# Scores of a pair ahead of the turn before it, and split multiply-adds, in the attention stages of a two-layer hybrid block

## The reference

```
def block(qi):                                   # global attention
    s = jnp.einsum('bqgrd,bkgd->bgrqk', qi, k_all).astype(jnp.float32) * d ** -0.5
    p = jax.nn.softmax(s, axis=-1).astype(v_all.dtype)
    return jnp.einsum('bgrqk,bkgd->bqgrd', p, v_all)
...
y = g[:, :, 0] * (branches[0] @ w_branch[0])     # merge
for i in range(1, N_BRANCH):
    y = y + g[:, :, i] * (branches[i] @ w_branch[i])
return y @ w_out
...
mod = jax.nn.silu(c) @ w_mod[l] + b_mod[l]       # modulation of a layer
```

## Time and profile before

| | us |
|---|---|
| median of 3 runs | 2744.23 |
| lowest and highest | 2742.33, 2746.5 |
| the profiled execution | 2742.03 |
| its span | 2740.4 |

### The profile page before, as it was taken

The page is one execution under the profiler, slowest core; times in us unless marked ns, Lnnn a source line. Parts: engine busy times, 40 slices in busy tenths (PEclk is TensorE's granted clock), DMA queues, the critical chain, the costliest instruction groups (busy, mean ns, idle before and its releaser), DMA issues.

```text
span 2740.4 us, 45413 instructions
## 1 busy us (share of the span) xinstructions
PE 2502.4 (91%) x19000; PEld 1530.5 (56%) x19001; DVE 1038.0 (38%) x2398; ACT 491.3 (18%) x978; POOL 231.8 (8%) x391
## 2 busy tenths in 40 slices
PE   7999999999998969999999999999999878888874
PEld 3455545454443457777777655667676544444442
DVE  2226536256465342222222251636457432111112
ACT  2023222222222011111111021323222111101110
POOL 3000001000000001111111110000000011111111
PEclk9989999999999979999999999999999979999997
DMA  9111118242324359999999762123465769999994
GB/s 293 61 62 62 47 43 305 114 142 85 112 87 131 125 193 370 370 374 381 378 383 387 292 203 92 62 77 104 145 185 179 257 265 409 410 418 413 415 404 169
DMA packets 153139, 616.72 MB, mean 225 GB/s; under 512 B 17121, under 2 KB 21489, under 8 KB 136465
## 3 DMA queue, kind: packets, MB, share of 16 engines
q1 hardware_dynamic: 126850, 557.88, 54.4%
q0 software_dynamic: 26192, 57.51, 6.5%
HBM read 598.37 MB, written 46.31 MB: 235 GB/s over the span
## 4 chain that ended last, share of the span: by engine, by line
PE 71%; DMA 15%; DVE 9%; issue 2%; ACT 2%; POOL 0%; DVEq 0%; SPq 0%; POOLq 0%; ACTq 0%
DMA ring<-in_e_down_dram 14%; PE bank L1660 13%; PE bank L1396 12%; PE bank L1288 11%; PE bank L1278 7%; PE score_banks L1677 4%; PE bank L1409 4%; PE score_banks L1697 3%; PE score_banks L1682 2%; PE bank L1567 2%; PE score_banks L1445 2%; PE turned_banks L1455 2%; PE bank L1643 1%; PE bank L1469 1%; PE bank L1317 1%
## 5 line engine op out<-in xcount | busy, mean ns | idle before, releaser
L1660 PEld LDWEIGHTS bank<-scr,ring 128*64 128x64 f32 x8192 | 340.6, 137 | 14.2 <-issue 14.2
L1396 PE MATMUL bank<-HT,ring 128*128 128x512 f32 (+1 forms) x1024 | 347.4, 494 | 0.8 <-ACT scr L1004 0.4
L1660 PE MATMUL bank<-scr,ring 128*64 128x96 f32 x8192 | 346.7, 247 | 1.2 <-DVE scr L2382 1.2
L1288 PE MATMUL bank<-ring,HT 128*128 128x512 f32 (+1 forms) x800 | 303.0, 535 | 0.0
L1653 PE MATMUL bank<-ring,scr 128*64 128x256 f32 x2048 | 239.8, 388 | 44.5 <-DMA ring<-in_e_gate_dram 22.8
L1396 PEld LDWEIGHTS bank<-HT,ring 128*128 128x128 f32 x1024 | 192.1, 192 | 143.2 <-issue 130.9
L1288 PEld LDWEIGHTS bank<-ring,HT 128*128 128x128 f32 x800 | 151.6, 193 | 142.3 <-issue 136.3
L1653 PEld LDWEIGHTS bank<-ring,scr 128*64 128x64 f32 x2048 | 146.5, 139 | 141.4 <-DMA ring<-in_e_gate_dram 41.5
L1278 PE MATMUL bank<-HT,ring 128*128 128x512 f32 (+1 forms) x512 | 196.1, 542 | 1.8 <-ACT HT L1004 1.8
L1697 PE MATMUL score_banks<-ring,scr 128*64 128x512 f32 x512 | 133.7, 670 | 35.5 <-DMA ring<-in_e_down_dram 33.8
L1278 PEld LDWEIGHTS bank<-HT,ring 128*128 128x128 f32 x512 | 97.0, 192 | 91.9 <-issue 88.4
(11 more groups left out here) (267 smaller groups left out, 2715.7 us busy)
## 6 DMA issues: line engine op xcount, KB each, us to landing
ring<-in_e_up_dram SPq DMA_DIRECT2D x64, 2048.0 KB, 22.0
ring<-in_e_down_dram SPq DMA_DIRECT2D x64, 2048.0 KB, 20.9
ring<-in_e_gate_dram SPq DMA_DIRECT2D x64, 2048.0 KB, 21.2
ring<-in_w_in_dram SPq DMA_DIRECT2D x34, 2048.0 KB, 8.0
ring<-in_w_mod_dram SPq DMA_DIRECT2D x32, 1024.0 KB, 5.2
ring<-in_w_mod_dram SPq DMA_DIRECT2D x8, 2048.0 KB, 19.5
ys<-consts POOLq DMA_DIRECT2D x1, 12288.0 KB, 41.7
ring<-in_w_branch_dram SPq DMA_DIRECT2D x4, 2048.0 KB, 7.9
```

Of the source, the lines that this page charges most:

```text
L1288: m = pe.matmul(bank[:, 0:width], HT[:, k, t * P:t * P + P], w[:, k, 0:width], start=k == 0, stop=k == KT_D - 1)
L1396: m = pe.matmul(bank[:, 0:NQ], w[:, k, (ft % 4) * P:(ft % 4) * P + P], HT[:, k, 0:NQ], start=k == 0, stop=k == KT_D - 1)
L1660: m = pe.matmul(ps[bank][rows_, f * cap:f * cap + cap], w[:, k, f * P + hf * HALF:f * P + hf * HALF + HALF], XTv[:, k, :], start=k == 0, s ...
```

## The change

On TensorE scores(i) now stands ahead of turn(i-1) in each step. On VectorE the part of the modulation sums that belongs to a step is cut in two by a new function `piece`: up to two multiply-adds (none in the first step of a block) go between peaks(i) and normalise(i), the rest stays at the end of the step. No wait is added or removed.

```diff
                     for i in range(n + 1):
+                        if i < n:
+                            scores(i)
                         if i:
                             turn(i - 1)
-                        if i < n:
-                            scores(i)
...
+                    def piece(b, i, late):
+
+                        for j in range(len(sum_blocks(l, b))):
+                            first, last = sum_span(l, b, j)
+                            ops, width = sum_list(l, b, j), last - first
+                            if not first <= i < last:
+                                continue
+                            part = ops[len(ops) * (i - first) // width:len(ops) * (i - first + 1) // width]
+                            early = 0 if i == first else min(2, len(part) // 2)
+                            part = part[early:] if late else part[:early]
+                            if part:
+                                accumulate(b, j, part)
+
                     for i in range(n + 1):
                         if i < n:
                             peaks(i)
+                            piece(b, i, 0)
                             normalise(i)
...
-                        for j in range(len(sum_blocks(l, b))):
-                            first, last = sum_span(l, b, j)
-                            ops, width = sum_list(l, b, j), last - first
-                            part = ops[len(ops) * (i - first) // width:len(ops) * (i - first + 1) // width] if first <= i < last else []
-                            if part:
-                                accumulate(b, j, part)
+                        piece(b, i, 1)
```

## The result

| | before | changed |
|---|---|---|
| median, us | 2745.36 (4 runs, 2742.33 to 2749.89) | 2702.2 (4 runs, 2698.78 to 2706.89) |
| the profiled execution | 2742.03 | 2698.78 |
| its span | 2740.4 | 2697.3 |
| granted TensorE clock of it | 0.959 | 0.961 |

The ratio is 0.9841, 95% interval 0.9824 to 0.9859: 43.2 us faster, where 31.6 was forecast. The kind of change was right and its size was a quarter too small.

The account below looks back on a forecast made before the run. TensorE, busy 91% of the span, was taken to bound the kernel; shorter waits and regained clock sum to 31.6 us, so 2742.0 becomes 2710.4, plus 2.2 for the median 2712.6, say 2713 us; range 2705 to 2732.

Parts of the forecast that it names:

- The idle terms: The waits to be removed in stages D, B and C of both layers, without the clock: 27.4 us.
- Scores followed by a turn never occur in before: TensorE's new neighbour order in 66 swapped steps, absent from the earlier trace; its price or gain was taken as 0.
- Its two bounds: Order on TensorE: losing a 0.07 us overlap in 66 steps costs 4.6 us, gaining as much is possible.
- the rule: Trainium skill: a weight load overlaps running matmuls only if they use other row groups; would make the gain smaller, not followed.
- three of its slow stretches: Stage C of layer 0: three stretches at lowered TensorE clock return to the upper level, 1.4 us each, 4.2.
- four places: Start of D, second long wait there, the 4.82 us wait, the 3.3 of layer 1: clock assumed to stay low.
- rival B: The clock stays up everywhere, also where the forecast left it slow: up to 8 us more, 2705 us; chance 0.05.
- the start of D: Layer 0: first turn waits 3.96 us, following group 2.03 for ScalarE; scores first to give 3.0, clock left slow.
- the 4.82: Longest turn wait, in C of layer 0, 4.82 us: only 1.1 was to go, and its clock to stay low.
- The turn's entry: TensorE's waits before a pair's transposes for VectorE's division, 38.7 us in 21 pieces; forecast to fall to about 10.
- Rival A: A new wait replaces the old as VectorE stays behind: gain only 12 to 16.6 us, 2727.6 to 2732; chance 0.23.

Follow-up runs that it names:

- scores first alone: Kernel before with only TensorE's list changed, scores(i) ahead of turn(i-1), multiply-adds left at the step's end: 2721.95 us against 2745.78, ratio 0.9916.

## Why the prediction was right, and where it was wrong

**Right.** That TensorE's idle time bounds the kernel and that the turn's waits are what the edit reaches: all 42.9 us are in the six stages. The idle terms (27.4 forecast, 24.0 measured), by stage: D 5.2 against 3.9, B 4.7 and 4.7, C 9.7 and 8.6, layer 1 7.8 and 6.8 (1.9, 1.6 and 3.3). The 0.6 us that the values' wait grows by in three steps of C: 0.63 each. That no multiply-add waits for its block: L2043 has no wait for a transfer. That multiply-adds beside exponentials cost nothing: the median L2043 takes 747 ns in both kernels, an exponential (L1165) 677 and 676. That scores to turn takes less than 1.2 us for a wide pair: 1.06. That the experts' stages take as long and only start earlier.

**Wrong, first: "Scores followed by a turn never occur in before ... I take 0".** The order was worth about 6.6 us (1.8 of them measured alone, in B of layer 0). Its two bounds, 4.6 us either way, came from the overlap of 0.07 us of two neighbours, and the value lies outside them. That overlap was also misread as a hidden load ("so I do not follow the rule"): at turn to scores and at scores to group the load starts together with its matmul, 0.00 us ahead, though the rows overlap by 0.07; where it is hidden, from turn to group, they overlap by 0.16 (1.09 busy, 0.93 apart). The rows that price it were there: a turn behind a dense group takes 0.97 us to the next start and 1.02 behind values, and its weight load starts 0.43 us early behind the group and not at all behind values. I looked at the edges that the new order makes, of which before has none, and not at the edges that it takes away or at the loads. Of the 44 edges from scores to a group in layer 0, each with an exposed load, the edit removed 41.

**Wrong, second: the clock, "three of its slow stretches stay at the upper level, 1.4 each: 4.2".** It is 10.7. I counted it in one stage only and left four places slow (rival B had them at up to 8 us together). Most of those recovered in part: the group behind the start of D took 8.80 us and takes 7.10, the one behind the 4.82 took 8.74 and takes 7.73. Waits that only became shorter give back clock too. Rival B had the second error's size nearly right (8 against 6.5) and a chance of 0.05, which was too low: there was no reason in the rows why a wait cut from 3.96 to 2.85 should keep its whole price.

**The sum.** Forecast 31.6; add 6.6 for the order and 6.5 for the clock, take off 3.4 for the waits: 41.3, against 42.9 in the stages and 43.2 of the medians. Had the two terms been right, the forecast would have been within 2 us.

**Smaller misses.** The turn's entry was to fall to about 10 us; it is 2.5, and the 12.4 stand under the scores' name, which the text did not foresee (14.9 together). L2195 and L2196 were to lose 32 of their 72 waits for ScalarE; they lost 15 (17 and 40 are left). Their waiting time fell from 101.1 to 64.8 us. The gate groups of C were to take 7.13 us; behind a turn they take 7.03, and one, behind the longest wait, 7.73. Rival A, "VectorE stays behind", is what scores first alone does (waits in B from 4.7 to 3.3); with the multiply-adds early it didn't happen.

**What stays open.** Order and clock come to 17.3 of the 18.9 us of busy time; the rest isn't explained. 0.6 of it is in C of layer 1, which lost 1.2 us at a clock of 1.00 in both, where the loads give 0.6. B of layer 0 gained 0.6 us and not the 0.9 that the rows give when scores went beside values. The order's value was measured apart from waits and clock in two stages only; for the others it is the estimate from their steps. Why a load isn't started early where the shape changes, no run here shows.

## What to carry to other kernels

When an edit only reorders a saturated TensorE, list the pairs of neighbours that it makes and that it removes, and look in the weight-load rows for which of them hide a load (here those of the same shape); with dozens of repetitions a load of 0.19 us is a term of the sum. Price a wait with the slow matmuls behind it, and let that price shrink with the wait. Work that is moved into another engine's gap should be about as long as the gap: less leaves arrears, more delays whoever waits at its end.

## What the runs showed of the hardware that was not expected

- A weight load starts early (0.03 to 0.43 us ahead of its first matmul) only between two neighbours of the same shape, both 128*128 or both 128*64 (28 places before, 54 changed); where the shape changes it starts with its matmul (172 of 172 and 147 of 147). A turn of 8 transposes takes 1.02, 0.97, 0.93 or 0.87 us to the next start with no dense group beside it, one ahead, one behind, or both.
- Useless transposes in nine waits made the kernel 11.4 us faster: behind the longest the granted clock was 1.00 instead of 0.66, and a turn took 1.09 us instead of 1.97.
- After about the same wait (1.88 and 1.97 us) at the same place the clock fell in one execution and not in the other.
